# A two-block transformer kernel on one core: where norms and filler matmuls stand in the program order

## The chip, the cores and the metric

The kernel runs on one core of one Trainium2 chip. The metric is device time in microseconds (us), lower is better, as the median of several executions of the whole program.

## The reference

One sequence of 256 tokens, 1024 features, float32, passes through two different blocks. Cut to what the change touches:

```python
# first block
h = rms_norm(x, g_pre_mix);  proj = h @ w_in          # q, k, v (512 each), q_lat 256, kv_lat 128, k_rope 32
o_sb  = stick_breaking_attention(sb_q, sb_k, sb_v)     # 8 heads
q  = rms_norm(q_lat, g_q_lat) @ w_q_up                 # the latent norms
kv = rms_norm(kv_lat, g_kv_lat) @ w_kv_up
o_mla = mla_attention(...)                             # 8 heads, causal softmax
mix = concatenate([rms_norm(o_sb, g_grp_sb), rms_norm(o_mla, g_grp_mla)]) @ w_o   # the group norms
...                                                    # feed-forward 2816 with conv, gated embedding
# second block (mod = silu(c) @ mod_w + mod_b, 1024 x 6144)
y_conv, y_att, y_pool = ...                            # sparse attention: 8 heads, softmax; pooling mixer
mix = concatenate([y_conv, y_att, y_pool]) @ w_out
x = x + g1 * mix
x = x + g2 * _hier_moe(rmsnorm(x) ...)                 # 32 experts, all weights read (201 MB)
```

## The kernel before, in words

Every engine has one queue written out by hand in program order: `pe`, `act`, `dve`, `pool` and `sp` (the last issues the DMAs). An instruction that waits holds up all that stands behind it on its engine. `chain` is a group of accumulating matmuls into one PSUM bank; `read[b]` is the token of the last reader of bank b, which the next writer waits for. Weights come through a ring of seven 2 MB slots (`stream`), loaded in program order; a load waits until the earlier user of its slot has freed it.

Activations lie features-on-partitions, 256 tokens wide. A norm is: squares on ScalarE, sums over partitions by a matmul with ones on TensorE, a square root on ScalarE (`Sqrt`, which needs another activation table than `Exp`), a reciprocal and a scaling on VectorE. `norm_scale` does one norm of the latents. `group_sums` does the sums of a wide norm in four row groups and copies them to `sd` with ScalarE; `wide_factor` calls it, adds the four groups up with one more matmul (the broadcast), and takes root and reciprocal.

In the first block the value projection is a loop over two halves of the tokens (`j`), eight matmuls of 128x512 each, whose result ScalarE copies out (`a_copy` to `vS`). The two latent norms stand behind the loop. Then come the scores of head pairs 2 and 3 of the stick-breaking attention (`sb_scores`).

Both softmax attentions run through `softmax_heads`, over four pairs of heads: `part1(i)` is scores, mask, maxima, exponentials and normalisation of pair i; `part2(i)` transposes the probabilities and copies them back with ScalarE; `part3(i)` multiplies with the values. Between them stand fillers, `fill(0)` to `fill(6)`, independent matmul work for TensorE. The order is a written list of (step, pair), step 0 a filler:

```python
for step, i in ((1, 0), (1, 1), (0, 0), (2, 0), (0, 1), (1, 2), (3, 0), (0, 2), (2, 1), (0, 3), (1, 3), (3, 1),
                (0, 4), (2, 2), (0, 5), (3, 2), (2, 3), (0, 6), (3, 3)):
```

Scores of pair i use banks 2(i mod 2) and the next one, so `part1(3)` waits until ScalarE has copied out `part2(1)`. In the first block the fillers (`mla_fill`) are slots of the modulation matrix (`mod_slot`, eight matmuls of 32x512), its first total (`mod_total(0)`, four small matmuls and an addition on VectorE, through bank 5), and the group norm of the first attention (`sb_group`, also bank 5). Behind them, fillers and the next stage split weights and activations in a high and a low part (`out_low`, `out_parts`) for the output projection (`wo_part`). In the second block the fillers (`dsa_fill`) are the router's bias row (eight matmuls of 128x36), the pooling mixer (two matmuls of 128x256, two copies on ScalarE) and four pieces of the output projection (`wout2`, four matmuls of 128x256 each). After the second attention come the rest of the output projection, the router and the experts: 96 slots of 2 MB, of which six are loaded before the second attention ends; the next ones wait for `t_arena`, the end of that attention, or for ring slots that the experts' matmuls free.

Of the kernel before, what the change touches and what calls it, by code (L numbers as in the profile page):

```python
# [10 lines left out]
ALU = mybir.AluOpType  # L11
ACT = mybir.ActivationFunctionType
AX = mybir.AxisListType

S = 256
# [72 lines left out]
def build(nc, A, out):  # L88
    with ExitStack() as ctx:
# [106 lines left out]
        def a_copy(o, i, *w, scale=1.0):  # L196
            return act(lambda e: e.activation(o, i, ACT.Copy, scale=scale), *w)  # L197
# [51 lines left out]
        def group_sums(b, squares, which):  # L249

            nt = len(squares)
            for k, (x, tok) in enumerate(squares):
                q = 32 * (k % 4)
                t = mm(ps[q:q + 32, b, 0:S], ones[:, 0:32], x, k < 4, k >= nt - 4, tok, read[b] if k < 4 else None, d_con,
                       inc=int(k == nt - 1))
            return a_copy(sd[:, which, :], bank(b, 0, S), t)

        def wide_factor(b, squares, which, dim, r):

            t = group_sums(b, squares, which)  # L260
            t = mm(bank(b, S, 512), ones, sd[:, which, :], True, True, t, inc=1)
            read[b] = t = a_fn(sd[:, which, :], bank(b, S, 512), ACT.Sqrt, t, t_eps, bias=eps, scale=1.0 / (32 * dim))
            return dve(lambda e: e.reciprocal(r, sd[:, which, :]), t)
# [75 lines left out]
        b = 0  # L339
# [173 lines left out]
        for j in range(2):  # L513
            b = 7 - j
            t = chain(bank(b), [(hT[:, k * S + 128 * j:k * S + 128 * (j + 1)], w.ap(k * 512, 512), th[k]) for k in range(8)],
                      w.ready, read[b])
            read[b] = a_copy(ar[:, vS + 512 * j:vS + 512 * (j + 1)], bank(b), t, t_rc, scale=rcol[:, j:j + 1])
            t_v.append(read[b])
        w.free(t)


        r, t_r = norm_scale(lat[:, 0:512], 2, 256, 0, t1, b=4)
        r2, t_r2 = norm_scale(lat[:, 512:768], 1, 128, 1, tk, b=5, at=1024)
        t_qn = apply_norm(ar, lat, lambda k: col("g_q_lat", k), 2, r, t_r, at=qn)
        t_kvn = v_stt(ar[:, kvn:kvn + S], lat[:, 512:768], col("g_kv_lat"), r2, ALU.mult, ALU.mult, t_r2)
        soft_tables()
# [51 lines left out]
        read[OB[1]] = a_copy(oT[:, 512:1024], bank(OB[1]), pv_done[3])  # L578
        t_osb.append(a_fn(ar[:, 512:1024], oT[:, 512:1024], ACT.Square, read[OB[1]]))

        def softmax_heads(score_pair, mask_pair, scale, v, t_vv, bufs, small, fill=None):


            sbuf, pbuf = bufs
            turned, done = {}, {}
            ptok = {}

            def part1(i):
                b = 2 * (i % 2)
                t = score_pair(i, b)  # L590
                s = sbuf[i % 2]
                t = mask_pair(i, b, s, t, turned.get(i - 2))
                m = small[:, (i % 2) * 16:(i % 2) * 16 + 16]
                s2 = as2(s)
                t1 = dve(lambda e: e.tensor_reduce(m[:, 0:2], s2[:, :, 0:128], AX.X, ALU.max), t, ptok.get(i - 2))
                t2 = dve(lambda e: e.tensor_reduce(m[:, 2:4], s2[:, :, 128:384], AX.X, ALU.max), t)  # L596
                t3 = v_ts(m[:, 4:8], m[:, 0:4], -scale, None, ALU.mult, None, t1, t2)
                te = []
                for par in range(2):
                    for lo, hi, c in ((0, 128, par), (128, 384, 2 + par)):  # L600
                        x = s[:, par * 384 + lo:par * 384 + hi]
                        te.append(a_fn(x, x, ACT.Exp, t3, bias=m[:, 4 + c:5 + c], scale=scale,
                                       accum_out=m[:, 8 + c:9 + c]))
                t4 = dve(lambda e: e.reciprocal(m[:, 12:16], m[:, 8:12]), te)
                tn = []
                for par in range(2):
                    for lo, hi, c in ((0, 128, par), (128, 384, 2 + par)):
                        x = s[:, par * 384 + lo:par * 384 + hi]
                        tn.append(v_ts(x, x, m[:, 12 + c:13 + c], None, ALU.mult, None, t4))
                ptok[i] = tn  # L610

            def part2(i):
                b = 2 * (i % 2)
                s = sbuf[i % 2]
                for par in range(2):
                    for n, lo in ((0, 0), (1, 128), (2, 256)):
                        x = s[:, par * 384 + lo:par * 384 + lo + 128]
                        o = ps[:, b + par, n * 128:n * 128 + 128]
                        t = pe(lambda e, x=x, o=o: e.transpose(o, x, ident), ptok[i], read[b], read[b + 1],  # L619
                               inc=int(par == 1 and n == 2))  # L620
                turned[i] = t
                p = pbuf[i % 2]
                read[b] = read[b + 1] = a_copy(as2(p), two(b), t, done.get(i - 2))
                turned[10 + i] = read[b]

            def part3(i):
                done[i] = weighted(i, pbuf[i % 2], v, turned[10 + i], t_vv, OB[i // 2])

            for step, i in ((1, 0), (1, 1), (0, 0), (2, 0), (0, 1), (1, 2), (3, 0), (0, 2), (2, 1), (0, 3), (1, 3), (3, 1),
                            (0, 4), (2, 2), (0, 5), (3, 2), (2, 3), (0, 6), (3, 3)):  # L630
                if step:
                    (part1, part2, part3)[step - 1](i)
                elif fill:
                    fill(i)
                if (step, i) == (3, 1):
                    yield done[1]
            yield done[3]
# [16 lines left out]
            return t  # L654

        small = misc[:, 16:48]
        tg = []

        def sb_group():
            r = rb[:, 0, :]  # L660
            t_r = wide_factor(5, [(tile(ar, k), t_osb[k // 2]) for k in range(4)], 0, 512, r)
            tg.extend(apply_norm(hT, hT, lambda k: col("g_grp", k), 4, r, t_r))

        OX, OW = (0, 2048), [4096, 5120] + [7680 + 1024 * k for k in range(6)]
# [10 lines left out]
        def out_parts(n, k, low, *waits):  # L675
            i = o_n[0] % 8
            o_n[0] += 1
            h, l = fr[:, OW[i]:OW[i] + 512], fr[:, OW[i] + 512:OW[i] + 1024]
            wo[n, k] = i, h, l, split(w_o[n].ap(512 * k, 512), h, l, low, w_o[n].ready, o_free[i], *waits)

        def mla_fill(i):
            if i == 0:
                mod_slot(0)
                mod_slot(1)
            elif i < 4:
                mod_slot(1 + i)
            elif i == 4:
                mod_total(0)
                sb_group()
            else:  # L690
                mod_slot(i)
            if i == 6:
                w_o.extend([stream("wo", j) for j in range(2)])
                for k in range(4):
                    out_low(k, tg[k], v_tt, t_mla[0])
                    out_parts(0, k, v_tt if k % 2 else p_tt, t_mla[0])

        t_om = []
        for j, t in enumerate(softmax_heads(mla_scores, mla_mask, 96 ** -0.5, vm, t_vm,
# [582 lines left out]
        def wout2(i, ks, last=False):  # L1282
# [6 lines left out]
                    started.add(b)  # L1289
            return t  # L1290

        def dsa_fill(i):
            if i == 0:
                for k in range(8):
                    t = mm(ps[:, 4, 0:36], sh[:, k:k + 1].broadcast_to([128, 128]), rw3[:, k, :], k == 0, k == 7,
                           t_mod, t_rw, read[4], inc=int(k == 7))
                read[4] = v_tt(rbias, ps[:, 4, 0:36], col("router_b", 0, 36), ALU.add, t, d_cols)
                t_rb.append(read[4])
            elif i == 1:
                for c in range(2):  # L1300
                    t = chain(bank(5, S * c, S * c + S), [(pw[:, 128 * c:128 * c + 128], tile(ar, c, pmx), t_pm)], t_rw, read[5])
                t_arena.append(t)
                for c in range(2):
                    mixed[c] = t_mix[c]
                    mixed[6 + c] = a_fn(tile(yT, 6 + c), bank(5, S * c, S * c + S), ACT.Copy, t, t_dn, scale=col("pool_scale", c))
                read[5] = mixed[7]
            elif i in (2, 3):
                wout2(0, (0, 1) if i == 2 else (6, 7))
            elif i in (4, 5):
                wout2(1, (0, 1) if i == 4 else (6, 7))  # L1310

        t_rb, t_arena = [], []
        OB = (6, 7)
        t_at = []
        for j, t in enumerate(softmax_heads(dsa_scores, dsa_mask, 0.125, vd, t_vd,
                              [[pair(o, i) for i in range(2)] for o in (sA, wT)], small, dsa_fill)):
            read[OB[j]] = a_copy(yT[:, 512 + 512 * j:1024 + 512 * j], bank(OB[j]), t, t_ckv)
            mixed[2 + 2 * j] = mixed[3 + 2 * j] = read[OB[j]]
            t_at.append(read[OB[j]])
# [680 lines left out]
```

How the kernel before makes its waits and increments, by code:

```python
    def emit(self, eng):  # L65
        seen = {}
        def wait(w):
            if w is None:
                return
            if isinstance(w, list):
                for x in w:
                    wait(x)
                return
            sem, v = w
            if v > seen.get(id(sem), 0):
                eng.wait_ge(sem, v)
                seen[id(sem)] = v
        for waits, fn, sem, by in self.items:
            for w in waits:
                wait(w)
            ins = fn(eng)
            if sem is not None:
                ins.then_inc(sem, by)
# [1744 lines left out]
            def run(e):  # L1830
                e.wait_ge(*t_flag)
                reg = e.alloc_register()
                e.reg_load(reg, flag[0:1, 0:1])
                with e.If_ne(reg, 0):
                    for s_, n in ends:
                        e.wait_ge(s_, n)
                    over.emit(e)
                    e.wait_ge(*t_end)
# [8 lines left out]
        @block.sync  # L1847
        def _(e):
            sp.emit(e)
            e.wait_ge(s_out, 64)
```

## Time and profile before

| what | value |
|---|---|
| time, median of 3 | 994.34 us (993.92 to 997.03) |
| profiled execution: its own time | 995.91 us |
| profiled execution: span, first to last instruction | 994.1 us |
| TensorE matmul busy | 813.6 us (82%) |
| VectorE, ScalarE, GpSimd busy | 331.9, 309.9, 143.9 us |
| granted TensorE clock, mean | 0.928 |
| chain that ended last | PE 53%, DMA 33%, DVE 6%, ACT 5% |
| HBM read | 296 MB, 299 GB/s over the span |

The span is what the profile shows from the first to the last instruction; the execution's own time is 1.8 us more. PE is TensorE, DVE VectorE, ACT ScalarE, POOL GpSimd, SP the engine that issues the DMAs. A float32 matmul leaves two records, so x16 in a row is eight matmuls of the source. A clock of 1.00 is 2.4 GHz and 0.50 is 1.2 GHz.

### The profile page before, as it was taken

The numbers are of one execution on the slowest core, as the hardware profiler recorded it, in microseconds if no ns is written. First come the engines' busy times: TensorE is split into PE (matmuls) and PEld (weight loads), VectorE is DVE, ScalarE is ACT, GpSimd is POOL, SyncE is SP. The second block draws the span as 40 slices with busy tenths as digits, with TensorE's granted clock in tenths as the row PEclk, the third lists the DMA queues.
The fourth block names the chain that finished last, engine by engine and source line by source line (L and its number), as shares of the span: only waits on it lengthen the run. The fifth ranks groups of instructions, "written<-read, shape, count | busy, mean of one in ns | idle before, by whom it ended". The sixth has DMA issues, their size and how long they took to land.

```text
span 994.1 us, 12347 instructions
## 1 busy us (share of the span) xinstructions
PE 813.6 (82%) x5144; PEld 528.1 (53%) x5144; DVE 331.9 (33%) x700; ACT 309.9 (31%) x621; POOL 143.9 (14%) x153
## 2 busy tenths in 40 slices
PE   7998879999999999999889998767666775665854
PEld 5856447899997886687768542213112221221212
DVE  3306465667676545559531310001000000100001
ACT  2316355666665556645541300000100000000001
POOL 0011013344443005135400000000000000000000
PEclk9999989999999999999989999879989688889779
DMA  9932964454553566733809799999999999999994
GB/s 359 428 113 82 396 273 169 157 183 170 183 197 109 220 216 218 294 143 116 307 1 404 263 398 396 428 431 426 429 428 427 429 428 428 428 427 427 430 428 201
DMA packets 23677, 297.93 MB, mean 300 GB/s; under 512 B 2752, under 2 KB 3008, under 8 KB 5440
## 3 DMA queue, kind: packets, MB, share of 16 engines
q1 hardware_dynamic: 23616, 297.09, 74.1%
q8 instruction: 42, 0.69, 0.3%
q14 instruction: 19, 0.16, 0.0%
HBM read 296.03 MB, written 1.05 MB: 299 GB/s over the span
## 4 chain that ended last, share of the span: by engine, by line
PE 53%; DMA 33%; DVE 6%; ACT 5%; POOL 1%; issue 1%; SPq 0%; DVEq 0%; POOLq 0%
PE ps L186 53%; DMA ring<-in_exps 32%; ACT ar L200 1%; POOL ar L217 1%; DVE ar L206 1%; ACT yT L200 1%; DVE fr L206 1%; ACT ar L197 1%; DMA ring<-in_win 1%; DVE yT L214 0%; ACT fr L197 0%; DVE misc L596 0%; ACT sq L200 0%; DVE yT L206 0%; PE ps L619 0%
## 5 line engine op out<-in xcount | busy, mean ns | idle before, releaser
L186 PE MATMUL ps<-ring,sq 128*32 128x512 f32 x976 | 138.1, 703 | 71.0 <-DMA ring<-in_exps 70.7
L186 PE MATMUL ps<-ring,ar 128*32 128x512 f32 (+3 forms) x792 | 106.7, 629 | 51.6 <-DMA ring<-in_exps 44.5
L186 PE MATMUL ps<-fr 128*128 128x256 f32 (+1 forms) x852 | 144.9, 325 | 4.7 <-DVE fr L206 4.3
L186 PEld LDWEIGHTS ps<-fr 128*128 128x128 f32 x852 | 124.9, 190 | 20.3 <-DVE fr L206 4.1
L186 PEld LDWEIGHTS ps<-ring,sq 128*32 128x32 f32 x976 | 29.7, 119 | 169.1 <-DMA ring<-in_exps 113.3
L186 PE MATMUL ps<-hT,ring 128*128 128x256 f32 (+2 forms) x416 | 93.3, 385 | 6.8 <-DMA ring<-in_win 6.8
L206 DVE TENSOR_TENSOR ar<-ar,ps 128x512 f32<-128x512 f32 x9 | 6.2, 688 | 253.7 <-PE ps L186 253.7
L186 PEld LDWEIGHTS ps<-hT,ring 128*128 128x128 f32 (+2 forms) x416 | 78.1, 189 | 20.8 <-DMA ring<-in_win 6.8
L186 PEld LDWEIGHTS ps<-ring,ar 128*32 128x32 f32 (+1 forms) x792 | 28.0, 121 | 112.4 <-DMA ring<-in_exps 69.7
L186 PE MATMUL ps<-ar 128*128 128x512 f32 (+9 forms) x320 | 72.8, 462 | 14.8 <-DVE ar L206 8.9
L206 DVE TENSOR_TENSOR fr<-ring,fr 128x512 fp32r<-128x512 f32 x79 | 65.1, 842 | 44.2 <-ACT fr L197 44.0
L197 ACT ACTIVATE ar<-ps 128x512 f32<-128x512 f32 (+5 forms) x49 | 27.6, 565 | 164.3 <-PE ps L1625 140.4
L206 DVE TENSOR_TENSOR ar<-ps,ar 128x512 f32<-128x512 f32 (+5 forms) x36 | 23.2, 660 | 137.3 <-PE ps L186 137.0
L186 PEld LDWEIGHTS ps<-ar 128*128 128x128 f32 (+4 forms) x320 | 40.4, 193 | 52.9 <-issue 21.8
L186 PE MATMUL ps<-fr,fr_h 128*128 128x256 f32 x528 | 67.4, 284 | 0.0
L186 PEld LDWEIGHTS ps<-fr,fr_h 128*128 128x128 f32 x528 | 65.4, 192 | 0.0
L200 ACT ACTIVATE sq<-ps,misc 128x128 f32<-128x128 f32 x31 | 11.9, 456 | 170.6 <-PE ps L186 170.6
L197 ACT ACTIVATE fr<-ring 128x512 fp32r<-128x512 f32 x98 | 57.3, 624 | 18.6 <-PE ps L186 18.5
L1511 POOL TENSOR_TENSOR ar<-ar 128x128 f32<-128x128 f32 x16 | 6.4, 399 | 373.2 <-DVE ar L206 372.4
L200 ACT ACTIVATE ar<-ps 128x768 f32<-128x768 f32 (+1 forms) x21 | 15.1, 717 | 107.6 <-PE ps L186 103.0
L197 ACT ACTIVATE fr_h<-ring 128x512 fp32r<-128x512 f32 x66 | 40.0, 625 | 18.1 <-PE ps L186 17.9
L206 DVE TENSOR_TENSOR fr_h<-ring,fr_h 128x512 fp32r<-128x512 f32 x43 | 31.7, 737 | 26.1 <-ACT fr_h L197 26.1
(194 smaller groups left out, 931.8 us busy)
## 6 DMA issues: line engine op xcount, KB each, us to landing
ring<-in_exps SPq DMA_DIRECT2D x90, 2048.0 KB, 30.7
ring<-in_modw SPq DMA_DIRECT2D x12, 2048.0 KB, 8.2
ring<-in_wup SPq DMA_DIRECT2D x11, 2048.0 KB, 8.8
ring<-in_win SPq DMA_DIRECT2D x5, 2048.0 KB, 9.2
ring<-in_wdown SPq DMA_DIRECT2D x5, 2048.0 KB, 8.3
ar<-in_exps SPq DMA_DIRECT2D x3, 2048.0 KB, 12.4
ring<-in_wo SPq DMA_DIRECT2D x2, 2048.0 KB, 10.1
ring<-in_wgate SPq DMA_DIRECT2D x2, 2048.0 KB, 8.5
```

The costliest lines, as they stand in the source:

```text
L186: return pe(lambda e: e.matmul(o, l, r, start=start, stop=stop, skip_group_check=True), *waits, inc=inc)
L197: return act(lambda e: e.activation(o, i, ACT.Copy, scale=scale), *w)
L200: return act(lambda e: e.activation(o, i, f, **kw), *w)
L206: return dve(lambda e: e.tensor_tensor(o, a, b, op), *w)
L217: return pool(lambda e: e.tensor_tensor(o, a, b, op), *w)
L1511: t_SG[g].append(pool(lambda e, o=o, x=x, gb=gb: e.tensor_tensor(o, x, gb, ALU.mult), tG, t_S[g], t_turned.get(g - 2)))
```

## The change

Three edits, none of which adds or removes arithmetic:

1. The two latent norms (sums, roots, reciprocals) are called inside the value projection's loop, after the matmuls of the first half and before its copy.
2. `wide_factor` is split: `group_sums` of the group norm stands in filler 4, the rest (`wide_root`: broadcast, root, reciprocal) and the scaling in filler 5, behind `mod_slot(5)`. `mod_total(0)` moves from filler 4 to the end of filler 6.
3. In the second block the pooling mixer moves between the scores of pair 0 and pair 1 (`early`), the router's row goes to bank 7, and the pieces of `wout2` move from fillers 2, 3, 4, 5 to fillers 0, 1, 2, 4.

```diff
@@ wide_factor
-            t = group_sums(b, squares, which)
+            return wide_root(b, which, dim, r, group_sums(b, squares, which))
+
+        def wide_root(b, which, dim, r, t):
+
             t = mm(bank(b, S, 512), ones, sd[:, which, :], True, True, t, inc=1)
             read[b] = t = a_fn(sd[:, which, :], bank(b, S, 512), ACT.Sqrt, t, t_eps, bias=eps, scale=1.0 / (32 * dim))
             return dve(lambda e: e.reciprocal(r, sd[:, which, :]), t)
@@ value projection
+            if j == 0:
+                r, t_r = norm_scale(lat[:, 0:512], 2, 256, 0, t1, b=4)
+                r2, t_r2 = norm_scale(lat[:, 512:768], 1, 128, 1, tk, b=5, at=1024)
             read[b] = a_copy(ar[:, vS + 512 * j:vS + 512 * (j + 1)], bank(b), t, t_rc, scale=rcol[:, j:j + 1])
             t_v.append(read[b])
         w.free(t)
-        r, t_r = norm_scale(lat[:, 0:512], 2, 256, 0, t1, b=4)
-        r2, t_r2 = norm_scale(lat[:, 512:768], 1, 128, 1, tk, b=5, at=1024)
@@ softmax_heads
                 if step:
                     (part1, part2, part3)[step - 1](i)
+                    if early and (step, i) == (1, 0):
+                        early()
@@ sb_group, mla_fill
-        def sb_group():
+        def sb_group(t):
             r = rb[:, 0, :]
-            t_r = wide_factor(5, [(tile(ar, k), t_osb[k // 2]) for k in range(4)], 0, 512, r)
+            t_r = wide_root(5, 0, 512, r, t)
@@
             elif i == 4:
-                mod_total(0)
-                sb_group()
+                t_gs.append(group_sums(5, [(tile(ar, k), t_osb[k // 2]) for k in range(4)], 0))
+            elif i == 5:
+                mod_slot(5)
+                sb_group(t_gs[0])
             else:
-                mod_slot(i)
+                mod_slot(6)
             if i == 6:
...
+                mod_total(0)
@@ dsa_early, dsa_fill
+        def dsa_early():
+            for c in range(2):
+                t = chain(bank(5, S * c, S * c + S), [(pw[:, 128 * c:128 * c + 128], tile(ar, c, pmx), t_pm)], t_rw, read[5])
...
         def dsa_fill(i):
             if i == 0:
                 for k in range(8):
-                    t = mm(ps[:, 4, 0:36], sh[:, k:k + 1].broadcast_to([128, 128]), rw3[:, k, :], k == 0, k == 7,
+                    t = mm(ps[:, 7, 0:36], sh[:, k:k + 1].broadcast_to([128, 128]), rw3[:, k, :], k == 0, k == 7,
...
+                wout2(0, (0, 1))
             elif i == 1:
...
-            elif i in (2, 3):
-                wout2(0, (0, 1) if i == 2 else (6, 7))
-            elif i in (4, 5):
-                wout2(1, (0, 1) if i == 4 else (6, 7))
+                wout2(1, (0, 1))
+            elif i in (2, 4):
+                wout2(i // 2 - 1, (6, 7))
```

The first place is ScalarE at the value projection. In the rows, `ar<-ps,misc 128x512` are the copies of the two value halves, `sq<-yT` the squares of the latents, `sd<-ps,misc` their roots, and `ar<-ps 128x768` is the first step of the scores of pair 2. Before:

```order
L197 ACTIVATE ar<-ps,misc 128x512 x2
L200 ACTIVATE sq<-yT 128x512
L200 ACT_TABLE_LOAD
L200 ACTIVATE sd<-ps,misc 128x256
L200 ACTIVATE sq<-yT 128x256
L200 ACTIVATE sd<-ps,misc 128x256
L364 ACT_TABLE_LOAD
L200 ACTIVATE ar<-ps 128x768
```

Now:

```order
L200 ACTIVATE sq<-yT 128x512
L200 ACT_TABLE_LOAD
L200 ACTIVATE sd<-ps,misc 128x256
L200 ACTIVATE sq<-yT 128x256
L200 ACTIVATE sd<-ps,misc 128x256
L197 ACTIVATE ar<-ps,misc 128x512 x2
L367 ACT_TABLE_LOAD
L200 ACTIVATE ar<-ps 128x768
```

The squares, the first table load and the roots now stand ahead of both copies; the number of table loads is the same. On TensorE the three sums (`ps<-sq,con 128x256 x3`) moved from behind the sixteen value matmuls to behind the first eight.

The second place is TensorE in the first block's softmax attention, from the values of pair 1 on. `con,ar 128x4` is `mod_total(0)`, `ar,con 32x256` the group norm's sums, `sd,con` its broadcast, `con,yT` are transposes, `ring,ar 32x512` is a `mod_slot`. One piece of the difference:

```order
+L186 MATMUL ps<-ar,con 32x256 x4
+L623 MATMUL ps<-con,yT 128x128 x6
+L186 MATMUL ps<-ring,ar 32x512 x8
+L186 MATMUL ps<-sd,con 128x256
+L186 MATMUL ps<-ar 64x256
+L186 MATMUL ps<-ar 64x128
+L186 MATMUL ps<-ar 64x256
+L186 MATMUL ps<-ar 64x128
+L623 MATMUL ps<-con,yT 128x128 x6
+L186 MATMUL ps<-ring,ar 32x512 x8
 L186 MATMUL ps<-con,ar 128x4 x4
-L186 MATMUL ps<-ar,con 32x256 x4
```

The sums come at once, transposes and a modulation slot stand between them and the broadcast, and the total comes last.

The third place is TensorE in the second block's attention, from the last scores of pair 1 to those of pair 2. `ar,misc 128x36` is the router's row, `con,ar` are transposes of pair 0, the two `ar 128x256` behind them the pooling mixer, `yT,ring` a `wout2` piece. Before:

```order
L186 MATMUL ps<-ar 128x256
L186 MATMUL ps<-ar,misc 128x36 x8
L619 MATMUL ps<-con,ar 128x128 x6
L186 MATMUL ps<-ar 128x256 x2
L186 MATMUL ps<-ar 128x128
```

Now:

```order
L186 MATMUL ps<-ar 128x256
L186 MATMUL ps<-ar,misc 128x36 x8
L186 MATMUL ps<-yT,ring 128x256 x4
L623 MATMUL ps<-con,ar 128x128 x6
L186 MATMUL ps<-yT,ring 128x256 x4
L186 MATMUL ps<-ar 128x128
```

Two pieces of the output projection now stand ahead of the scores of pair 2, where the router's row and the mixer stood alone; ahead of the scores of pair 3 one piece is left where two were.

## Rows read from the trace of the kernel before

**Rows 1.** The page: mean busy share of the DMA engines in 40 slices.

```profile
DMA  9932964454553566733809799999999999999994
```

**Rows 2.** Busy time by stretch: us, each engine's busy time, granted clock, DMA share, GB/s.

```profile
506.00:520.00 14.00, 12.77 (x81) 10.01 (x79) 4.98 (x16) 6.40 (x20) 0.00 (x0) 1.00 0.01 1
...
601.00:980.00 379.00, 250.51 (x1638) 83.98 (x1630) 26.01 (x63) 21.58 (x49) 3.99 (x10) 0.85 1.00 425
```

**Rows 3.** Timeline of the DMA issues after the second attention: start, us, operation.

```profile
520.95 1.28 SPq L150 DMA_DIRECT2D ar<-in_exps  x3
```

**Rows 4.** Timeline of PE, value projection to the scores of pair 2.

```profile
58.91 13.90 PE L186 MATMUL ps<-ring,hT 128*128 128x512 f32 x32
74.10 1.13 PE L186 MATMUL ps<-sq,con 128*128 128x256 f32 x4 [1.30 <-ACT sq L200]
...
76.82 3.18 PE L186 MATMUL ps<-ar 64*128 64x256 f32 x32
```

**Rows 5.** Timeline of ACT in the same stretch.

```profile
65.98 0.69 ACT L197 ACTIVATE ar<-ps,misc 128x512 f32<-128x512 f32 x1 [6.06 <-PE ps L186]
...
75.73 0.41 ACT L200 ACTIVATE sq<-yT 128x256 f32<-128x256 f32 x1
...
77.42 1.28 ACT L364 ACT_TABLE_LOAD   x1
78.72 0.81 ACT L200 ACTIVATE ar<-ps 128x768 f32<-128x768 f32 x1
```

**Rows 6.** Timeline of PE in the first softmax attention, behind the values of pair 1.

```profile
128.13 1.08 PE L186 MATMUL ps<-ar,con 128*32 128x256 f32 x8 [3.91 <-DVE misc L206]
...
139.24 1.85 PE L186 MATMUL ps<-fr 128*128 128x512 f32 x6 [0.42 <-POOL fr L217]
```

**Rows 7.** Timeline of ACT there.

```profile
127.15 0.63 ACT L200 ACTIVATE sq<-hT 128x512 f32<-128x512 f32 x1
...
130.98 0.47 ACT L200 ACTIVATE sd<-ps,misc 128x256 f32<-128x256 f32 x1
...
136.20 0.81 ACT L197 ACTIVATE sq<-ps 128x768 f32<-128x768 f32 x1 [3.13 <-PE ps L619]
136.91 0.41 ACT L197 ACTIVATE fr<-hT 128x256 fp32r<-128x256 f32 x1
```

**Rows 8.** Timeline of DVE there.

```profile
127.91 0.17 DVE L206 TENSOR_TENSOR misc<-ps,cols 128x16 f32<-128x16 f32 x1
131.48 1.75 DVE L263 RECIPROCAL rb<-sd 128x256 f32<-128x256 f32 x1 [3.40 <-ACT sd L200]
133.27 1.67 DVE L214 SCALAR_TENSOR_TENSOR hT<-hT,cols,rb 128x256 f32<-128x256 f32 x4
```

**Rows 9.** Timeline of POOL there.

```profile
137.92 1.27 POOL L217 TENSOR_TENSOR fr<-ring,fr 128x512 fp32r<-128x512 f32 x1 [47.99 <-ACT fr L197]
```

**Rows 10.** Timeline of PE in the second block's attention.

```profile
496.65 1.51 PE L619 MATMUL ps<-con,ar 128*128 128x128 f32 x6 [2.69 <-DVE ar L210]
...
501.33 4.22 PE L186 MATMUL ps<-ar 128*128 128x128 f32 x16 [1.47 <-ACT ar L197]
505.48 1.99 PE L186 MATMUL ps<-yT,ring 128*128 128x256 f32 x8
...
509.69 2.28 PE L186 MATMUL ps<-ar 128*128 128x128 f32 x16
...
516.61 0.88 PE L186 MATMUL ps<-ar 128*64 128x256 f32 x8 [0.33 <-ACT ar L197]
```

**Rows 11.** Timeline of ACT there: the copy of pair 1's transposed probabilities.

```profile
508.38 0.79 ACT L197 ACTIVATE ar<-ps 128x768 f32<-128x768 f32 x1
```

**Rows 12.** Timeline of DVE there: the masks of pairs 2 and 3.

```profile
504.30 0.96 DVE L206 TENSOR_TENSOR ar<-ps,ar 128x768 f32<-128x768 f32 x1 [2.25 <-PE ps L186]
...
511.21 0.96 DVE L206 TENSOR_TENSOR ar<-ps,ar 128x768 f32<-128x768 f32 x1 [1.38 <-PE ps L186]
```

**Rows 13.** Busy time by stretch, columns as in rows 2.

```profile
127.00:133.00 6.00, 4.36 (x20) 2.22 (x24) 2.60 (x6) 3.64 (x6) 0.00 (x0) 0.50 0.54 229
...
495.00:505.00 10.00, 6.89 (x22) 4.92 (x24) 5.23 (x16) 3.42 (x13) 0.00 (x0) 0.50 0.04 18
```

More of the change, by code:

```diff
@@ L579, in build, with softmax_heads @@
         t_osb.append(a_fn(ar[:, 512:1024], oT[:, 512:1024], ACT.Square, read[OB[1]]))
-        def softmax_heads(score_pair, mask_pair, scale, v, t_vv, bufs, small, fill=None):
+        def softmax_heads(score_pair, mask_pair, scale, v, t_vv, bufs, small, fill=None, early=None):
             sbuf, pbuf = bufs
@@ L656, in build @@
         small = misc[:, 16:48]
-        tg = []
-        def sb_group():
+        tg, t_gs = [], []
+        def sb_group(t):
             r = rb[:, 0, :]
-            t_r = wide_factor(5, [(tile(ar, k), t_osb[k // 2]) for k in range(4)], 0, 512, r)
+            t_r = wide_root(5, 0, 512, r, t)
             tg.extend(apply_norm(hT, hT, lambda k: col("g_grp", k), 4, r, t_r))
@@ L1290, in wout2 @@
             return t
+        def dsa_early():
+            for c in range(2):
+                t = chain(bank(5, S * c, S * c + S), [(pw[:, 128 * c:128 * c + 128], tile(ar, c, pmx), t_pm)], t_rw, read[5])
+            t_arena.append(t)
+            for c in range(2):
+                mixed[c] = t_mix[c]
+                mixed[6 + c] = a_fn(tile(yT, 6 + c), bank(5, S * c, S * c + S), ACT.Copy, t, t_dn, scale=col("pool_scale", c))
+            read[5] = mixed[7]
         def dsa_fill(i):
@@ L1294, in dsa_fill @@
                 for k in range(8):
-                    t = mm(ps[:, 4, 0:36], sh[:, k:k + 1].broadcast_to([128, 128]), rw3[:, k, :], k == 0, k == 7,
-                           t_mod, t_rw, read[4], inc=int(k == 7))
-                read[4] = v_tt(rbias, ps[:, 4, 0:36], col("router_b", 0, 36), ALU.add, t, d_cols)
-                t_rb.append(read[4])
-            elif i == 1:
[L1300 to L1306, printed above, removed]
-            elif i in (2, 3):
-                wout2(0, (0, 1) if i == 2 else (6, 7))
-            elif i in (4, 5):
-                wout2(1, (0, 1) if i == 4 else (6, 7))
+                    t = mm(ps[:, 7, 0:36], sh[:, k:k + 1].broadcast_to([128, 128]), rw3[:, k, :], k == 0, k == 7,
+                           t_mod, t_rw, read[7], inc=int(k == 7))
+                read[7] = v_tt(rbias, ps[:, 7, 0:36], col("router_b", 0, 36), ALU.add, t, d_cols)
+                t_rb.append(read[7])
+                wout2(0, (0, 1))
+            elif i == 1:
+                wout2(1, (0, 1))
+            elif i in (2, 4):
+                wout2(i // 2 - 1, (6, 7))
         t_rb, t_arena = [], []
@@ L1315, in build @@
         for j, t in enumerate(softmax_heads(dsa_scores, dsa_mask, 0.125, vd, t_vd,
-                              [[pair(o, i) for i in range(2)] for o in (sA, wT)], small, dsa_fill)):
+                              [[pair(o, i) for i in range(2)] for o in (sA, wT)], small, dsa_fill, dsa_early)):
             read[OB[j]] = a_copy(yT[:, 512 + 512 * j:1024 + 512 * j], bank(OB[j]), t, t_ckv)
```

## The prediction

> **What bounds the kernel now.** I read the share of the DMA engines over the span first. It is patchy up to slice 20 and then stays at 9 from slice 23 on, with one 7 between [rows 1]. The table by stretch says the same: from 601 to 980 us the DMA engines are busy all the time at 425 GB/s, and TensorE works 251 of those 379 us [rows 2]. So the second half is the experts' weight stream, and nothing in it can be won by matmul order. The question is when that stream begins. Between 506 and 520 us the DMA engines do nothing (share 0.01) while TensorE is busy 12.8 of 14 us [rows 2]; the next load of expert weights is issued at 520.95 [rows 3], on the token that closes the second attention. The stream dips again around slice 22 until the first experts' matmuls free ring slots, and those too stand behind the attention, the output projection and the router on TensorE. The reader is to see two regimes: a chain of compute up to about 560 us, and a stream of fixed length behind it. A microsecond won anywhere on the chain moves the stream's restart and the end by a microsecond. All three edits lie on the first part.
>
> Next I read the timelines of the three places engine by engine, for which wait ends last in each.
>
> **Edit 1, the latent norms.** Before, the sixteen value matmuls run from 58.91 to 72.81. TensorE then idles 1.30 us for the squares of the latents, does the sums, and starts the scores of pair 2 at 76.82 [rows 4]. ScalarE does not begin those scores' first step until 78.72, because a table load of 1.28 us stands ahead of it [rows 5]. ScalarE was idle for 6.06 us before 65.98 [rows 5], and the latents had long been written; so in the new order squares (under 0.7 us) and the load of the root's table are done by about 62, ahead of the first half's end at 58.91 + 13.90/2 = 65.86. The 1.30 us of idle goes. The rest of the piece, 76.82 − 74.10 = 2.72 us with one inner wait for the second square (0.41 us, [rows 5]) and the root ahead of it, is kept: 65.86 + 2.72 + 6.95 = 75.53 for the scores of pair 2. On ScalarE the last value copy (0.69) and one table load (1.28) follow the second half: 75.53 + 0.03 + 0.69 + 1.28 = 77.53 against 78.72, so 1.2 us. The sums' pipeline fill (1.13 us for two matmuls [rows 4], against 1.99 us for four of the same width in a run [rows 10]) may overlap the value matmuls, which would make it 1.5. **I take 1.3 us; bounds 0.5 and 1.7.** The low bound is for the case that the mid-projection wait grows. The reciprocals come earlier on VectorE, ahead of anything urgent. The weight slot of the value projection is freed 2.7 us later, which delays a load of the modulation matrix that is used only in filler 5, 50 us on; that costs nothing.
>
> **Edit 2, the group norm.** Behind the values of pair 1 TensorE idles 3.91 us [rows 6]. It waits for bank 5, which `mod_total(0)`'s addition on VectorE releases, and that addition stood behind the normalisation of pair 3 and ran at 127.91 [rows 8]. The new order has no such wait: the sums can run at 128.13 − 3.91 = 124.22, then transposes (0.85 us) and a modulation slot (1.92 us), to about 127.0. What is late next is ScalarE: the copy of the sums stands behind the exponentials of pair 3 and the square that ends at 127.15 + 0.63 = 127.78 [rows 7]. So: sums copied by 128.2, the copy of pair 2's transposes 0.81 (like the one of [rows 7]) to 129.0, table load 1.28 ([rows 5]) to 130.3, root 0.47 ([rows 7]) to 130.8. VectorE: reciprocal 1.75 to 132.6, first scaled tile 1.67/4 to 133.1 [rows 8]. The broadcast, the values of pair 2 and the transposes of pair 3 fit in beside that, and the copy of pair 3's transposes ends at about 131.6. Before, that copy was waiting for TensorE until 136.20, and the first split of the normalised tile stood behind it at 136.91 [rows 7]. It will be at 133.1: 3.8 us earlier. From there the chain is unchanged: split, GpSimd's low part (1.27 us [rows 9]), first matmul of the output projection, 139.24 [rows 6], to 135.4. TensorE has its own work done before that: slot 6 to 132.6, the total 1.1 and the values of pair 3 0.9, to 134.6. The weights of these slots were issued some 30 us ahead. `mod_total(0)` now stands behind filler 6's low parts on VectorE, and bank 5 is next wanted some 4 us later; nothing waits. **I take 3.8 us; bounds 2.5 (a further wait of TensorE's pieces for ScalarE) and 3.9, all of the idle time.**
>
> In this stretch the clock stood at half from 127 to 133 [rows 13]; it had fallen during the 3.91 us of idle. The new gap there is about 1.2 us. But since the new chain runs over ScalarE and VectorE, the clock adds nothing to the term.
>
> **Edit 3, the second attention.** The scores of pair 2 begin at 501.33 in both orders: they wait for ScalarE's copy of pair 0, which stands behind the exponentials of pair 1, and those depend on VectorE, not on fillers. What changes is the clock. TensorE idled 2.69 us before 496.65 and 1.47 us before 501.33 [rows 10], and the clock stood at half from 495 to 505 [rows 13]. The same sixteen records took 4.22 us at 501.33 and 2.28 us at 509.69, when it was back [rows 10]. So the mask of pair 2 started 504.30 − 501.33 = 2.97 us after the scores' start, and that of pair 3 511.21 − 509.69 = 1.52 us [rows 12]. In the new order the mixer, the router's row and two `wout2` pieces (1.99 us each [rows 10]) fill TensorE until about 499.6; one gap of 1.7 us is left. If the clock stays up, the mask of pair 2 is 1.45 us earlier, and so are its exponentials and the copy of pair 1 behind them: 508.38 [rows 11] becomes 506.93, done by 507.7. The scores of pair 3 wait for that copy alone, since the piece of filler 3 that kept TensorE until 509.69 is gone: start 507.75, mask 509.27, against 511.21: 1.94 us. The last pair's chain, to the values and the rest of the output projection, follows it unchanged. If the clock is low there all the same, the scores of pair 3 start at 509.2 instead of 509.69: 0.5 us. **I take 1.95 us; bounds −1 and 2.5.** The low bound is worked out under the first rival. The mixer costs 0.9 us ahead of pair 1's scores, which VectorE cannot take up anyway before it has normalised pair 0 (that is what the 2.69 us of [rows 10] waited for), and its two ScalarE copies fall into idle time between the exponentials of pairs 0 and 1.
>
> One rule speaks against this edit. The Trainium skill ("TensorE: Matmul & The Clock Gate", section "A second HAM failure mode: psum-queue depth-cycling") says that short idles between groups of matmuls are enough to make the clock oscillate; the trace agrees so far as gaps of 2.69 and 1.47 us had it at half. By the rule, this edit would bring 0.5 us or less instead of 1.95, and the sum would be 5.6.
>
> **The sum.** 1.3 + 3.8 + 1.95 = 7.05 us. The profiled execution took 995.91 us (span 994.1); it would take 988.9. The median of the runs is 1.57 us below that execution, so the forecast is 994.34 − 7.05 = 987.3 us.
>
> **The rivals.**
>
> *The clock falls in the second attention in spite of the fillers.* For it: the new order leaves gaps of about 1.7 us before the scores of pair 2, 1.4 before those of pair 3, 1.8 before the values of pair 2 and 0.9 before the last ones, where before a late gap was only 0.33 [rows 10]; and the router's row is 1.9 us of matmuls of only 36 columns. Against it: all else is dense, and the gap of 2.69 is closed. Price: the first term of edit 3 falls to 0.5; if the clock falls in the late gaps, the rest of the output projection starts slow and gives up 1.5 us more. Total gain 4 to 5.6 us: 988.7 to 990.3 us.
>
> *The gains before 520 us do not reach the end.* If the stream were bound by its own order of loads rather than by the token at 520.95, edits 1 and 2 would be swallowed. Against it: DMA share 0.01 from 506 to 520 [rows 2]. It would leave 0 to 2 us: 992.3 to 994.3, within what a measurement of this kernel can tell from no change, about 0.3% or 3 us.
>
> *Slower, by the clock.* The fillers are taken from late gaps; if the clock falls at the end of the attention and stays low over the output projection, router and first experts, each microsecond of that work costs another one. The low stretch of before had 6.9 us of TensorE work in 10 us [rows 13], so it cost about 3.4. To eat 7.05 and lose 3 more, 10 us of full-rate work must run at half clock, 20 us on end from 518 on; then 997.4 us. Against it: that work has no gaps, and the clock came back at 505 once TensorE was busy.
>
> **How the numbers follow.** The forecast, 6 to 8.5 us won: 0.62, its own range 985.8 to 988.4. Clock rival: 0.25. Swallowed: 0.09. Slower: 0.04. The range of 8 in 10 takes in the first two cases and the runs' own spread, 984.6 to 990.8. Faster by over 0.3%: 0.87; within 0.3%: 0.09; slower: 0.04.
>
> **What the new profile would show.** Edit 1: no idle time for `sq` behind the sixteenth value matmul, one table load between the last value copy and pair 2's scores, and that step about 1.3 us earlier, near 77.4. Edit 2: no wait for `misc` before the group sums; a wait for `sd` of about 1.2 us before the broadcast; the first matmul of the output projection near 134.1 (139.24 less 5.1). Edit 3: clock 1.00 through the attention, with the expert loads issued 1.95 us sooner after the mask of pair 0 than before, at 513.9 (520.95 less 7.05). I am wrong if the clock column shows 0.50 there, if GpSimd's or ScalarE's part of the split has moved behind something else, or if the load's issue moves and the end does not.

## The result, and the profile after

The changed kernel takes 992.34 us (median of 20 runs, which lie between 990.69 and 999.66) against 995.35 us (20 runs, 993.20 to 1001.69): ratio 0.9967, 95% interval 0.9952 to 0.9982. By the ratio that is 3.3 us faster, 1.8 to 4.8. The forecast was 987.3 us, 7 us faster. Its profiled execution took 990.85 us, span 989.0: a lucky one, 1.5 us under its median, as before's was 0.6 above its own. The two spans differ by 5.1 us.

The value projection of the kernel after, TensorE (columns as in [rows 4]):

```profile
58.72 7.03 PE L186 MATMUL ps<-ring,hT 128*128 128x512 f32 x16
65.59 1.03 PE L186 MATMUL ps<-sq,con 128*128 128x256 f32 x4
67.48 0.70 PE L186 MATMUL ps<-sq,con 128*128 128x256 f32 x2 [0.87 <-ACT sq L200]
68.02 7.03 PE L186 MATMUL ps<-ring,hT 128*128 128x512 f32 x16
74.98 3.18 PE L186 MATMUL ps<-ar 64*128 64x256 f32 x32
```

and ScalarE behind the second half:

```profile
75.08 0.69 ACT L197 ACTIVATE ar<-ps,misc 128x512 f32<-128x512 f32 x1 [5.82 <-PE ps L186]
75.79 1.28 ACT L367 ACT_TABLE_LOAD   x1
77.08 0.81 ACT L200 ACTIVATE ar<-ps 128x768 f32<-128x768 f32 x1
```

The first sums have no wait now. From the start of the value projection to the scores' first step on ScalarE it is 77.08 − 58.72 = 18.36 us; before 78.72 − 58.91 = 19.81 [rows 4, 5].

The first softmax attention, TensorE:

```profile
122.91 1.92 PE L186 MATMUL ps<-ring,ar 128*32 128x512 f32 x16
126.48 0.70 PE L186 MATMUL ps<-sd,con 128*128 128x256 f32 x2 [1.64 <-ACT sd L197]
...
134.25 1.65 PE L186 MATMUL ps<-fr 128*128 128x512 f32 x6 [1.75 <-POOL fr L217]
...
170.84 4.44 PE L186 MATMUL ps<-fr 128*128 128x256 f32 x24 [1.57 <-DVE fr L206]
175.12 3.04 PE L186 MATMUL ps<-fr,fr_h 128*128 128x256 f32 x24
```

The wait of 3.91 us for `misc` [rows 6] is gone; one of 1.64 us for `sd` stands ahead of the broadcast, where about 1.2 was forecast. The output projection starts 4.99 us earlier. But look at 170.84: the up projection's first 24 records take 4.44 us, and the next 24, of the same shape, 3.04. The clock was down, in code that the change does not touch. The table by stretch of the same kernel (columns as in [rows 2]):

```profile
170.00:174.00 4.00, 3.16 (x15) 3.19 (x16) 3.91 (x12) 2.30 (x6) 0.00 (x0) 0.57 0.00 0
...
485.00:498.00 13.00, 10.46 (x62) 9.04 (x63) 7.34 (x21) 8.62 (x23) 1.41 (x2) 1.00 0.51 197
498.00:501.50 3.50, 3.50 (x15) 2.13 (x14) 1.90 (x4) 0.00 (x0) 0.00 (x0) 0.52 0.00 0
502.00:516.00 14.00, 10.15 (x68) 7.59 (x67) 4.52 (x14) 7.09 (x21) 0.00 (x0) 1.00 0.01 1
...
549.00:560.00 11.00, 9.06 (x61) 5.03 (x64) 5.09 (x25) 2.55 (x5) 1.60 (x4) 0.84 0.34 109
```

In the second attention the clock fell at 498, right where the scores of pair 2 run. The gap ahead of them, forecast at 1.7 us, is 2.11. TensorE there:

```profile
493.38 1.89 PE L186 MATMUL ps<-yT,ring 128*128 128x256 f32 x8
497.38 3.73 PE L186 MATMUL ps<-ar 128*128 128x128 f32 x16 [2.11 <-ACT ar L197]
...
504.82 2.39 PE L186 MATMUL ps<-ar 128*128 128x128 f32 x16 [0.90 <-ACT ar L197]
...
511.84 0.88 PE L186 MATMUL ps<-ar 128*64 128x256 f32 x8 [2.06 <-ACT ar L197]
```

The loads of the experts behind it, and the masks of pairs 2 and 3 on VectorE:

```profile
516.18 1.28 SPq L150 DMA_DIRECT2D ar<-in_exps  x3
```

```profile
499.66 0.96 DVE L206 TENSOR_TENSOR ar<-ps,ar 128x768 f32<-128x768 f32 x1 [1.57 <-PE ps L186]
...
506.44 0.96 DVE L206 TENSOR_TENSOR ar<-ps,ar 128x768 f32<-128x768 f32 x1 [1.25 <-PE ps L186]
```

From pair 0's mask to the load issue it took 29.16 us, against 29.98 before. So by stage the second profile differs from the first by −1.45 and −3.35 us for edits 1 and 2, −0.3 in the output projection, +1.3 in the up projection, +0.1 from there to the second attention, −0.8 in it, and −0.3 behind the issue; with a start 0.2 us earlier that is the −5.1. The stream did not swallow anything.

### The profile page after: what moved, and what is told of

Read it like the earlier page. It is cut to its first block, busy times and chain, and to the rows that moved or that the text cites. A ratio compares the mean times of both kernels' runs of the same rounds, so it can differ in the third digit from the quotient of the medians.

```text
span 989.0 us, 12352 instructions
## 1 busy us (share of the span) xinstructions
PE 806.6 (82%) x5144; PEld 525.1 (53%) x5144; DVE 331.3 (33%) x700; ACT 309.6 (31%) x621; POOL 144.2 (15%) x153
## 4 chain that ended last, share of the span: by engine, by line
PE 54%; DMA 32%; DVE 6%; ACT 5%; POOL 1%; issue 1%; SPq 0%; DVEq 0%; POOLq 0%
PE ps L186 54%; DMA ring<-in_exps 32%; ACT ar L200 1%; POOL ar L217 1%; DVE ar L206 1%; ACT yT L200 1%; ACT ar L197 1%; DVE fr L206 1%; DMA ring<-in_win 0%; DVE yT L214 0%; DVE misc L600 0%; DVE yT L206 0%; DVE rb L266 0%; DVE hT L214 0%; ACT fr L197 0%
## 5 line engine op out<-in xcount | busy, mean ns | idle before, releaser
L186 PE MATMUL ps<-ar 128*128 128x512 f32 (+9 forms) x320 | 67.2, 442 | 18.1 <-DVE ar L206 8.9
L206 DVE TENSOR_TENSOR ar<-ps,ar 128x512 f32<-128x512 f32 (+5 forms) x36 | 23.2, 660 | 130.9 <-PE ps L186 130.6
L186 PEld LDWEIGHTS ps<-ar 128*128 128x128 f32 (+4 forms) x320 | 37.6, 182 | 51.7 <-DVE ar L206 19.8
```

What stands on the lines that cost most here:

```text
L186: return pe(lambda e: e.matmul(o, l, r, start=start, stop=stop, skip_group_check=True), *waits, inc=inc)
L206: return dve(lambda e: e.tensor_tensor(o, a, b, op), *w)
```

## The experiments

Five stages are followed through all profiles: **L**, start of the value projection to the scores' first step on ScalarE; **G**, from there to the output projection's first matmul; **U**, the up projection's first tile to the load of `pT` behind it; **D**, pair 0's mask in the second attention to the load issue; and **E**, from the load issue to the first output. "Half clock at" lists where, up to 600 us, the granted clock fell to 0.50.

**The edits one by one.** Each kernel is the one before with one edit of the diff.

> Only edit 1 (latent norms between the halves). Theory A, each edit's saving reaches the end and falls of TensorE's clock give part of it back: the first score step of pair 2 is about 1.4 us earlier (77.3 instead of 78.72 from the span's start), the end 1.4 us earlier, give or take 1 to 2 us of clock luck: ratio 0.997 to 1.000. Theory B, savings before the experts' stream are swallowed: same shift at that step, but the load issue behind the second attention moves and the end does not.

> Only edit 2 (group norm's sums apart from broadcast, total moved). Theory A: the first matmul of the output projection 3.3 to 3.8 us earlier (135.4 to 135.9 instead of 139.24), the end 3 to 3.5 us earlier unless a half-clock stretch of 1.3 us falls into the start of the up projection: ratio 0.9955 to 0.998. Theory B: the step moves, the end stays within 1 us.

> Only edit 3 (fillers of the second attention). Theory A: from the mask of pair 0 to the load issue behind the attention 29.2 us (as in the changed kernel) if the clock falls again in the gap before the scores of pair 2, 28 us if it stays up; before it was 30.0. End 0.8 to 2 us earlier: ratio 0.998 to 0.9992. Theory C, the fillers do nothing but move the idle time: 0 to 0.8 us and a low clock somewhere in the attention in every execution.

| kernel | ratio, interval | L | G | U | D | E | half clock at |
|---|---|---|---|---|---|---|---|
| before, first profile | | 19.81 | 60.52 | 129.37 | 29.98 | 467.0 | 112, 126, 454, 495 |
| edit 1 | 0.9984 (0.9967 to 1.0001) | 18.37 | 61.34 | 131.85 | 29.60 | 465.0 | 127, 174, 499 |
| edit 2 | 0.9966 (0.9949 to 0.9983) | 19.81 | 58.79 | 130.82 | 30.15 | 464.9 | 120, 137, 175, 455, 496 |
| edit 3 | 1.0001 (0.9982 to 1.0020) | 20.16 | 61.29 | 129.30 | 29.17 | 466.7 | 78, 115, 129, 456, 504, 559 |
| after, first profile | 0.9967 (0.9952 to 0.9982) | 18.36 | 57.17 | 130.67 | 29.16 | 466.7 | 170, 450, 498, 552 |

L is 18.37 with edit 1 and 19.81 without it, 1.45 us; the 20.16 of edit 3 has half clock at 78 in it. Edit 2 carries the measured gain by itself: 3.4 us by its ratio. Edit 3 is worth 0.8 us in its stage; no gain shows in the time (−0.1 us, between −2.0 and 1.8). Theory B (swallowed) falls with edit 2's ratio. What remains odd: G varies by 0.8 us between the three executions with the old order and by 1.6 between the two with the new one, U by 2.5 us with the same code, and half-clock stretches lie in them where they are long.

**Filling the idle gaps.** If the clock is what varies, spare matmuls in the gaps should hold it.

```diff
+        def warm(b, n, cols=512):
+            for _ in range(n):
+                mm(bank(b, 0, cols), ones, con[:, 0:cols], True, True, read[b], d_con)
...
             elif i < 4:
+                if i == 3:
+                    warm(7, 3)
                 mod_slot(1 + i)
+                if i == 1:
+                    warm(7, 2)
...
                 mod_slot(5)
+                warm(7, 1)
...
+        warm(6, 1)
         for k in range(2):
             out_parts(1, k, v_tt, t_mla[0])
...
         t = over_rows(3, r, t_r, read[3])
+        warm(6, 1)
         tx = []
...
                 wout2(1, (0, 1))
+                warm(6, 2)
...
+            elif i == 3:
+                warm(7, 1, 256)
+            elif i == 5:
+                warm(7, 2)
```

> The changed kernel with ten spare matmuls of 512 columns and one of 256 (ones times constants, into free banks, results never read) in its idle gaps on TensorE in both softmax attentions and ahead of the up projection. If half-clock stretches are what ate the rest of the gain: granted clock 1.00 from 95 to 530 us, mask of pair 2 in the second attention 1.5 us after the start of its scores instead of 2.3, first six weight tiles of the up projection in 3.0 us instead of 4.4, end 2 to 2.5 us earlier than the changed kernel (ratio to before 0.993 to 0.995). If the clock is not the cause: the same as the changed kernel, 0.9967, or slower by the spare matmuls that do not fit their gap.

(There are twelve of 512 columns, not ten.) Ratio 0.9899 (0.9876 to 0.9922), median 987.57 us of six runs. The only half-clock stretch left up to 600 us is at 549, where no spare matmul stands. The profile shows what was expected: its span is 986.6 us against 989.0 of the changed kernel, 2.4 us less, in the stages where the clock had fallen. The ratio gives more, 6 to 7 us against the changed kernel's; that a usual execution loses more to the clock than the profiled one would explain it, but no row here shows it. The next three kernels tell what the edits are worth once the clock is up: `before_warm` puts fifteen such matmuls (not sixteen) in the gaps of the kernel before, `e12_warm` has edits 1 and 2 but not 3, `warm_att` pads the second attention of the changed kernel only.

```diff
             elif i == 4:
                 mod_total(0)
+                warm(7, 4)
                 sb_group()
...
                 t_rb.append(read[4])
+                warm(7, 3)
             elif i == 1:
...
                 read[5] = mixed[7]
+                warm(6, 2)
```

> The kernel before with spare matmuls in its own idle gaps (sixteen of 512 columns: in the first block's attention, ahead of the up projection, in the second attention), no edit. Theory A, clock luck hides the edits' own worth: granted clock 1.00 in both attentions and ahead of the up projection, time 4 to 5 us below the kernel before (ratio 0.995 to 0.9965), and the changed kernel with such matmuls (0.9899) is 5 to 6.5 us below this one. Rival, the spare matmuls are worth the whole 9.6 us and the edits nothing once the clock is up: ratio 0.990.

> Edits 1 and 2 with spare matmuls in both attentions and ahead of the up projection, the second attention's own fillers as before. It shows what edit 3 is worth when the clock stays up: the mask of pair 3 is then 0.5 us later than with edit 3, since one filler piece still keeps TensorE ahead of the scores of pair 3; from the mask of pair 0 to the load issue 28.7 us instead of 28.25; ratio 0.9904 against 0.9899. If edit 3's order is worth 1.95 us by itself: 0.992.

> The changed kernel with spare matmuls only in the second attention (four of 512 columns, one of 256). Theory A: clock 1.00 from 485 to 516, from the mask of pair 0 to the load issue 28.25 us instead of 29.16, end about 1 to 1.5 us earlier than the changed kernel (ratio 0.995 to 0.996), run-to-run spread still several us, because the other places are as before. If the attention were the place where nearly all was lost: 0.991.

| kernel | ratio, interval | G | U | D | E | half clock at |
|---|---|---|---|---|---|---|
| before_warm | 0.9957 (0.9938 to 0.9976) | 58.48 | 129.37 | 28.26 | 466.7 | 553 |
| e12_warm | 0.9928 (0.9902 to 0.9954) | 57.17 | 129.37 | 28.25 | 464.8 | none |
| warm | 0.9899 (0.9876 to 0.9922) | 57.17 | 129.32 | 28.25 | 466.8 | 549 |
| warm_att | 0.9943 (0.9919 to 0.9968) | 57.18 | 132.06 | 28.26 | 466.5 | 169, 552 |

The masks of pairs 0 to 3 in `before_warm`, whose fillers are in the old order:

```profile
488.54 0.96 DVE L210 TENSOR_TENSOR ar<-ps,ar 128x768 f32<-128x768 f32 x1 [1.25 <-PE ps L186]
493.98 0.95 DVE L210 TENSOR_TENSOR ar<-ps,ar 128x768 f32<-128x768 f32 x1
500.51 0.96 DVE L210 TENSOR_TENSOR ar<-ps,ar 128x768 f32<-128x768 f32 x1 [0.90 <-PE ps L186]
507.05 0.96 DVE L210 TENSOR_TENSOR ar<-ps,ar 128x768 f32<-128x768 f32 x1 [1.01 <-PE ps L186]
```

and in `warm`, in the new order:

```profile
485.35 0.96 DVE L210 TENSOR_TENSOR ar<-ps,ar 128x768 f32<-128x768 f32 x1 [1.26 <-PE ps L186]
490.79 0.95 DVE L210 TENSOR_TENSOR ar<-ps,ar 128x768 f32<-128x768 f32 x1
497.32 0.96 DVE L210 TENSOR_TENSOR ar<-ps,ar 128x768 f32<-128x768 f32 x1 [0.91 <-PE ps L186]
503.86 0.96 DVE L210 TENSOR_TENSOR ar<-ps,ar 128x768 f32<-128x768 f32 x1 [1.01 <-PE ps L186]
```

The spacings are the same to 0.01 us: 5.44, 6.53, 6.54. `warm` has a spare matmul where the piece of filler 3 stood, but `after_r` below, with the new order, no spare matmul and the clock up, has D 28.25 as well. So with the clock up the order of the fillers is worth nothing. My own expectation for `e12_warm`, D 28.7 instead of 28.25 for the piece in filler 3, was a miss.

In the first attention the same comparison, from the scores' first step to the output projection, is for `before_warm`

```profile
79.04 0.81 ACT L204 ACTIVATE ar<-ps 128x768 f32<-128x768 f32 x1
137.52 1.85 PE L186 MATMUL ps<-fr 128*128 128x512 f32 x6 [0.42 <-POOL fr L221]
```

and for `warm`

```profile
77.56 0.81 ACT L204 ACTIVATE ar<-ps 128x768 f32<-128x768 f32 x1
134.73 1.65 PE L186 MATMUL ps<-fr 128*128 128x512 f32 x6 [0.69 <-POOL fr L221]
```

It gives edit 2 58.48 − 57.17 = 1.31 us. The two spans, 989.7 and 986.6 us, differ by 3.1 us: 1.44 in L, 1.31 in G, 0.35 in the output projection, nothing in D. That is what the three edits save in the profiles with the clock up on both sides, against the 7.05 of the forecast.

The ratios are less sharp. Between `before_warm` and `warm` they differ by 5.8 us; and `e12_warm` has a higher ratio than `warm` (0.9928, with overlapping intervals, 0.9904 or 0.992 expected) though its profiled span, 984.4 us, is 2.2 us shorter. `warm_att`, with half clock at 169 all the same, has a ratio of 0.9943 against the changed kernel's 0.9967 and 0.9963 (below), but the intervals overlap and its median, 992.14 us, is the changed kernel's.

**Two more gaps.**

```diff
+        warm(7, 1)
         for j in range(2):
             t = mm(ps[:, 5, 8 * j:8 * j + 8], wit...
...
             over_tokens(i)
+        mm(bank(4), ones, xT[:, 0:512], True, True, read[4], tt)
```

> The changed kernel with the spare matmuls of the earlier run and two more: one ahead of the small transposes of the index weights (about 448 us), one beside the router's chain (about 547 us). If those places too fall to half clock in some executions: the up-front part loses its low stretches near 450 and 550 us, 0.5 to 1.5 us less: ratio 0.9885 to 0.9895. Otherwise 0.9899 again or up to 0.3 us slower.

There is no half-clock stretch up to 600 us, and E is 465.1. The ratio, 0.9925 (0.9896 to 0.9955), is not told apart from `warm` by these intervals; medians 988.32 and 987.57 us.

**Is it luck where the clock falls?** Both kernels again, unaltered.

> The changed kernel again, unaltered. Theory A, the half-clock stretches of one execution are luck and not set by the program: they stand elsewhere than in the first profile (170, 450, 498 and 552 us); the steps without one keep their length to 0.1 us (value projection's start to the first score step of pair 2 18.4, from there to the output projection 57.2, up projection 129.3, issue of expert loads to the first output 465.0 without a fall beside the router and 466.7 with one). Ratio 0.995 to 0.998. Rival, the edits bring about the fall ahead of the up projection: it is there again, with the part from its start to the next loads 130.7 to 132 us long.

> The kernel before again, unaltered, timed against itself: ratio 1.000, and the width of its interval shows what the timing can tell. Theory A: half-clock stretches elsewhere than at 112, 126, 454 and 495 us; the second attention from the mask of pair 0 to the load issue anywhere between 28.3 and 30.2 us by how much of it is at half clock.

`after_r`: 0.9963 (0.9948 to 0.9979), half clock at 110, 172 and 554; G 58.35, U 131.92, D 28.25 (no fall in the attention this time), E 466.6. Its eight runs lie within 2.2 us of each other (991.57 to 993.78), as close as the six of `warm`. `before_r`: 0.9988 (0.9974 to 1.0002), but its half-clock stretches stood at 112, 126, 453 and 494, just as in the first profile. That expectation failed. By then all five profiles with edit 1 or 2 and no spare matmul ahead of the up projection had a fall there, and none of the three without these two, so two more draws of the kernel before were taken.

> The kernel before, one more profile, for one question: the half-clock stretch ahead of the up projection stood in all five profiles with edit 1 or 2 and no spare matmuls, and in none of the three without them. If that is luck, kernel before shows it too in some execution: from the up projection's first tiles to the load behind it 130.6 to 132 us instead of 129.37. If the edits bring it about: 129.37 again.

> The same as before_r2, a second draw: 130.6 to 132 us in at least one of the two if it is luck, 129.37 in both if it is the edits. Half-clock stretches of the second attention: 28.3 to 30.2 us from the mask of pair 0 to the load issue.

U was 131.85 and 131.91, with half clock at 176 and at 180. So the fall ahead of the up projection comes without the edits too. Whether they make it more frequent is not settled: over all profiles without a spare matmul there, it stands in eight of eight with edit 1 or 2 (U 131.3 us on average) and in three of six without them (130.6). G was 62.87 and 63.89, D 29.60 and 29.61. `before_r2` by stretch:

```profile
178.00:183.00 5.00, 4.89 (x23) 4.93 (x24) 4.76 (x14) 3.02 (x7) 0.00 (x0) 0.50 0.00 0
...
501.00:508.00 7.00, 4.80 (x16) 3.08 (x16) 2.54 (x10) 3.27 (x11) 0.00 (x0) 0.51 0.00 0
```

**The fall beside the router.** The five profiles with edit 3 and no spare matmul at the router had half clock there and a longer E; of eight without edit 3, one had.

> Edits 1 and 2, no edit 3, no spare matmuls. Theory D, edit 3's own saving in the attention (about 0.9 us) is taken back beside the router, where all five profiles with edit 3 had a half-clock stretch that costs the stream 1.6 to 1.8 us, and one of eight without: no half-clock stretch beside the router, from the load issue to the first output 465.0 us, ratio 0.995 to 0.9965, no worse than the changed kernel. Theory A, plain luck: the stretch can stand there, and edit 3 is worth 0.9 us: ratio 0.996 to 0.998.

> The changed kernel with a single spare matmul (512 columns) beside the router's chain. Both theories: clock 1.00 there, issue to first output 465.0 us instead of 466.6. Time 1 to 1.8 us below the changed kernel (ratio 0.9945 to 0.9955) if the stretch stands there in most executions (D), 0.5 us or less if it is rare (A).

> Edit 3 alone, one more profile. D: half clock beside the router again, first output 466.5 to 466.8 us after the load issue. A: either.

> The changed kernel, a third profile. D: half clock beside the router again, first output 466.5 to 466.8 us after the load issue. A: either.

| kernel | ratio, interval | G | U | D | E | half clock at |
|---|---|---|---|---|---|---|
| e12 | 0.9960 (0.9945 to 0.9976) | 58.46 | 131.82 | 29.61 | 465.6 | 110, 171, 496 |
| after_router | 0.9958 (0.9943 to 0.9974) | 57.17 | 130.59 | 29.16 | 465.9 | 170, 450, 498 |
| e3_fill_r | one run | 63.33 | 131.87 | 28.25 | 466.5 | 76, 131, 179, 561 |
| after_r2 | one run | 57.16 | 130.60 | 29.16 | 466.5 | 170, 450, 498, 552 |

The third profile of the changed kernel and the second of edit 3 show the fall again. One spare matmul takes it away; by stretch, `after_r2` and then `after_router`:

```profile
545.00:560.00 15.00, 13.05 (x96) 9.02 (x99) 7.33 (x39) 5.56 (x11) 1.60 (x4) 0.89 0.46 170
```

```profile
545.00:560.00 15.00, 13.84 (x111) 9.76 (x111) 7.37 (x40) 5.39 (x11) 1.60 (x4) 1.00 0.58 223
```

E falls from 466.5 to 465.9, where 465.0 was expected, and the time by less than these intervals can tell. E is also 467.0 in two profiles of the kernel before without any fall there, so the stretch is not all that moves it. `e12`, without edit 3, cannot be told from the changed kernel in time, and has no fall beside the router.

## Why the prediction was wrong

**The bound** was read rightly: a saving ahead of the load issue reached the end. The rival that the gains do not reach it is refuted by edit 2's ratio alone (0.9966, interval 0.9949 to 0.9983).

**Edit 1, 1.3 us.** Right: 1.45 us between profiles without a fall in this stage, timed 1.6 with an interval of −0.1 to 3.3.

**Edit 2, 3.8 us.** The wait that goes and the one that comes in its place were right, and so was the size: G over the seven profiles without edit 2 and without spare matmuls in this attention averages 61.97 us, over the seven with it 57.75, 4.2 us less; the first pair of profiles gives 3.35. But the text says that "the clock adds nothing to the term", and that is wrong: the size came out right for a reason that the sum did not have. With the clock up in both orders the edit is worth 1.31 us. The rest is half-clock time. In all seven profiles of the old order the clock fell in the idle time of 3.9 us or just as it ended (between 126 and 131 us), ahead of transposes and a modulation slot on TensorE that ScalarE then waits for (3.13 us in [rows 7], 2.42 in `before_warm`). Edit 1's profile, which has this fall and no other in the stage, is 61.34 − 58.48 = 2.86 us longer in G than `before_warm`. In the new order four of the seven have no fall in the stage. My sum worked the after side with full clock and compared it with rows at half clock.

**Edit 3, 1.95 us.** This is the step that failed: the term of 1.95 us, of which the first profile after shows 0.8 in the stage and the run with edit 3 alone none in the time. I took that "the clock stays up" in the attention and that the scores of pair 3 would profit from the piece gone from filler 3. The clock fell there in four of six profiles with the edit and without spare matmuls in the attention, and D was 29.16 or 29.17 instead of 28.25; and the filler's place is worth nothing, since in `before_warm` D is 28.26 with the old fillers. Where the clock did stay up (`after_r`, `e3_fill_r`) the stage was 1.7 us shorter than before, close to the term. But that is a gain of clock, not of order, and no profile of the old order without spare matmuls had it. Averaged, the edit gives 0.9 us in its stage; no gain shows in the time (1.0001, interval 0.9982 to 1.0020), though the interval does not exclude 0.9 us. The first rival of the prediction, with a chance of 0.25, was this fall; its total gain of 4 to 5.6 us is nearer, but 992.34 us lies outside its 988.7 to 990.3 as well. The rule of the Trainium skill ("TensorE: Matmul & The Clock Gate", section "A second HAM failure mode: psum-queue depth-cycling"), that short idles between groups make the clock oscillate, was the better guide here. The trace agrees with it in those four of six profiles. With the 0.5 us that the prediction worked out for this case the sum was 5.6.

**What the sum left out.** Falls of the clock in places that the edits do not touch: ahead of the up projection 1.3 to 2.7 us, around 450 us 0.8 us, beside the router up to 1.8 us. They come and go between executions of one program, though not freely: two profiles of the kernel before had them at the same places (112, 126, 454 and 495 us), and so had two of the changed kernel (170, 450, 498 and 552). So a single profile is one draw: I took 995.91 us and its rows for the kernel, and a median of three runs, 994.34, for its time, where later medians of it were 995.35 to 997.15. About 1 us of the miss is this base.

**Still open.** The stage averages add up to 6.6 us, the timed gain is 3.3 to 3.7. All seven profiles with edit 3 and no spare matmul at the router have the fall beside it, against one of nine without edit 3; it takes back 0.6 to 1.8 us. Why edit 3 should go with it was not found. The up projection takes back 0.7 us on average (131.3 against 130.6). And the profiled executions are not the timed ones: the spans of the four profiles of the kernel before average 995.5 us, those of the three of the changed kernel 989.7, which is 5.9 us apart, where the timed ratios give 3.3 to 3.7. With a spread of 1.6 to 3.4 us in G alone, averages over so few profiles leave the rest uncertain.

**The best version** that came out is the changed kernel with thirteen spare matmuls, 987.57 us, 0.9899: the result nearest to the forecast, reached by what the forecast took for granted. It cannot be told from `warm_all` and `e12_warm` (988.32 and 988.73 us), whose intervals overlap with its own.

## What to carry to other kernels

Before pricing a reordering, look at the granted clock under every row that the sum uses, on both sides; a row at half clock is not the price of that work, and do not take for granted that a schedule with gaps left on TensorE holds its clock: here gaps of 1.6 and 2.1 us went with falls. Filling gaps with any matmul, useful or not, was worth as much here (4.3 us on the kernel before, by its ratio) as the three reorderings together. And take two or three profiles before reading differences of a microsecond from one.

## What the runs showed of the hardware

With gaps of 2.11 us and less the clock fell in some executions and not in others of the same program: the stage D of the changed kernel was 29.16, 28.25 and 29.16 us. The fall need not come inside the gap: in the first profile of the changed kernel the clock was at 1.00 until 498 and then at half under the scores that had started at 497.38, after the idle 2.11 us. Beside the router TensorE is busy 13.05 of 15 us in the busy column, with small matmuls and, in the first profile of the changed kernel, no gap over 0.79 us between 545 and 552, and still the clock fell there, at 552. One fall behind the idle 3.91 us of the first attention cost 2.86 us (edit 1's profile against `before_warm`).
